# Two blocks of products opened together per arriving input tile, and one home for the split weights, in a two-block fp32 network on one core

## The reference

```python
def first_block(x, p, ...):
    u = rms_norm(h, norm_mix_w[l])
    proj = u @ w_in[l]                    # 24 blocks of 128 columns
    ...                                   # RG-LRU branch, GLA branch
    h = h + jnp.concatenate([ya, yb], axis=-1) @ w_out[l]
    gate = jax.nn.sigmoid(rms_norm(h, ple_norm_w[l]) @ w_ple_gate[l] + b_ple_gate[l])
    h = h + gate * (p[l] @ w_ple_proj[l])
...
# second block, per layer: n = rmsnorm(x, g); h = n * (1 + scale) + shift; x = x + gate * mixer(h)
def conv_branch(h, w_in, dw, db, ln_g, ln_b, w_out):      # layers 0 and 3
    a, b, gate = jnp.split(h @ w_in, 3, axis=-1)
    y = depthwise_conv(a * jax.nn.sigmoid(b), dw, db)
    y = jax.nn.silu(layernorm(y, ln_g, ln_b))
    return (y * jax.nn.silu(gate)) @ w_out
# layer 1: rwkv_mixer (features, wkv scan, readout @ w_o); layer 2: attn_mixer (q, k, v, g = h @ w_in;
# softmax attention; (o * silu(g)) @ w_out)
```

## Time and profile before

| | us |
|---|---|
| median of 3 runs | 3019.34 (3016.89 to 3021.15) |
| the profiled execution | 3007.58 |
| its span | 3005.8 |
| TensorE matmul busy | 2610.2 (87%) |
| VectorE busy | 1748.8 (58%) |
| ScalarE busy | 1122.0 (37%) |
| GpSimd busy | 776.2 (26%) |

### The profile page before, as it was taken

The page is one execution under the profiler, slowest core; times in us unless marked ns, Lnnn a source line. Parts: engine busy times, 40 slices in busy tenths (PEclk is TensorE's granted clock), DMA queues, the critical chain, the costliest instruction groups (busy, mean ns, idle before and its releaser), DMA issues. The chain is left out here.

```text
span 3005.8 us, 65971 instructions
## 1 busy us (share of the span) xinstructions
PE 2610.2 (87%) x28252; PEld 2028.2 (67%) x28252; DVE 1748.8 (58%) x2951; ACT 1122.0 (37%) x1751; POOL 776.2 (26%) x437
## 2 busy tenths in 40 slices
PE   7896879998599997788888888678999999898987
PEld 5774658776487686677677777567778755476755
DVE  4646978977822675454554554354771066535995
ACT  4531332223333422444444443332442344333323
POOL 2322210001122123644444452122332300032111
PEclk9998989989698898899999999889999999999998
DMA  4214424432234455111111100324332200033431
GB/s 149 77 43 133 161 71 118 111 93 91 97 107 151 157 188 182 40 36 45 51 40 46 51 25 14 122 91 147 133 126 64 84 1 1 1 119 92 136 94 56
DMA packets 83662, 266.34 MB, mean 89 GB/s; under 512 B 11824, under 2 KB 12848, under 8 KB 82992
## 3 DMA queue, kind: packets, MB, share of 16 engines
q1 hardware_dynamic: 74160, 236.97, 24.8%
q10 hardware_dynamic: 9216, 25.17, 2.1%
HBM read 203.04 MB, written 36.70 MB: 80 GB/s over the span
## 5 line engine op out<-in xcount | busy, mean ns | idle before, releaser
L358 PE MATMUL ps<-h_parts_conv,w_parts_conv 128*128 128x512 f32 x3936 | 766.5, 356 | 83.7 <-DVE h_parts_conv L344 47.6
L358 PEld LDWEIGHTS ps<-h_parts_conv,w_parts_conv 128*128 128x128 f32 x3936 | 643.2, 193 | 212.9 <-issue 54.7
L358 PE MATMUL ps<-scratch_scan 64*64 64x64 f32 (+1 forms) x15936 | 379.8, 239 | 82.9 <-issue 44.5
L358 PEld LDWEIGHTS ps<-scratch_scan 64*64 64x64 f32 x15936 | 342.9, 140 | 127.5 <-issue 83.6
L355 ACT ACTIVATE scratch_scan<-ps 128x384 f32<-128x384 f32 x560 | 241.0, 493 | 370.5 <-PE ps L358 228.4
L358 PE MATMUL ps<-h_parts_attn,w_parts_attn 128*128 128x512 f32 (+1 forms) x1536 | 330.5, 374 | 19.9 <-DVE h_parts_attn L352 12.3
L352 DVE SCALAR_TENSOR_TENSOR scratch_conv<-scratch_conv,vec 128x256 f32<-128x256 f32 (+1 forms) x672 | 335.2, 572 | 0.5
L358 PEld LDWEIGHTS ps<-h_parts_attn,w_parts_attn 128*128 128x128 f32 x1536 | 264.6, 191 | 78.6 <-issue 15.2
L432 POOL TENSOR_TENSOR w_parts_conv<-ring,w_parts_conv 128x1024 fp32r<-128x1024 f32 x50 | 131.4, 2629 | 592.2 <-ACT w_parts_conv L355 592.2
L358 PE MATMUL ps<-h_parts_block,w_parts_block 128*128 128x512 f32 x960 | 243.7, 414 | 38.5 <-POOL w_parts_block L432 27.7
L358 PEld LDWEIGHTS ps<-h_parts_block,w_parts_block 128*128 128x128 f32 x960 | 189.4, 200 | 92.4 <-issue 42.8
(11 more groups left out here) (206 smaller groups left out, 3586.0 us busy)
## 6 DMA issues: line engine op xcount, KB each, us to landing
ring<-in_weights SPq DMA_DIRECT2D x311, 512.0 KB, 3.7
rwkv_spill<-scratch_conv ACTq DMA_DIRECT2D x64, 384.0 KB, 2.3
stream<-rwkv_spill SPq DMA_DIRECT2D x64, 384.0 KB, 4.0
scratch_conv<-scratch_conv SPq DMA_DIRECT2D x128, 103.1 KB, 2.2
scratch_conv<-scratch_conv SPq DMA_DIRECT2D x128, 67.4 KB, 2.0
x_spill<-stream SPq DMA_DIRECT2D x2, 3072.0 KB, 9.7
y_spill<-scratch_scan SPq DMA_DIRECT2D x8, 384.0 KB, 4.0
scratch_rwkv_out<-y_spill SPq DMA_DIRECT2D x8, 384.0 KB, 6.5
```

Source lines behind the costliest of these rows:

```text
L358: return nc.tensor.matmul(o, l, r, start=start, stop=stop)
```

## The change

**1. Two blocks opened together.** A new function `first_products` takes the place of the first two `tile_product` calls in ten stages: in1, out1, gate1, conv0, convout0, rkvg, rwkvout, attn, conv1, convout1. At step k it waits for input tile k, does block 0's tile k, and then block 1's tile k - lag, with a lag of 4 at width 512 and of 3 at width 768. What stood between the two blocks (in attn the spreading, in gate1 a small product) now stands behind both. attnout keeps its order.

**2. One home for the split weights.** `weight_parts` makes the tensor once for everything to rkvg, is closed for the scan, and makes it again at rwkvout for all that follows. So the limits of gate1, rwkvout, attn and attnout now reach two blocks into the next stage: these are rounded and parted in the tail of the stage before.

```diff
         def memory(name, split, room=ROOM, width=TT):
             parts_scope.close()
             area_scope.close()
+            if not split:
+                w_scope.close()
+                PARTS.pop("W")
+            elif "W" not in PARTS:
+                weight_parts(name)
...
         def parts(name, tiles, width):
             PARTS["H"] = ap(parts_scope.enter_context(nc.sbuf_tensor(f"h_parts_{name}", [P, 2, tiles, width], F32R)))
-            PARTS["W"] = ap(parts_scope.enter_context(nc.sbuf_tensor(f"w_parts_{name}", [P, 2, 2, DT * P], F32R)))
+
+        def weight_parts(name):
+            PARTS["W"] = ap(w_scope.enter_context(nc.sbuf_tensor(f"w_parts_{name}", [P, 2, 2, DT * P], F32R)))
...
+        def first_products(pe, outs, width, fresh, lag):
+            j0 = done["take"]
+            done["take"] += len(outs)
+            Hh, Hl = PARTS["H"][:, 0], PARTS["H"][:, 1]
+            for step in range(DT + lag):
+                if step < DT:
+                    pe.wait_ge(fresh[0], fresh[1] + fresh[2] * (step + 1))
+                for i, o in enumerate(outs):
+                    k = step - lag * i
+                    if not 0 <= k < DT:
+                        continue
+                    if k == 0:
+                        pe.wait_ge(parted, j0 + i + 1)
+                    W = PARTS["W"][:, (j0 + i) % 2].rearrange("p e (k m) -> p e k m", k=DT)
+                    product(o, W[:, 0, k, :], Hh[:, k, :], width, k == 0, False)
+                    product(o, W[:, 0, k, :], Hl[:, k, :], width, False, False)
+                    last = product(o, W[:, 1, k, :], Hh[:, k, :], width, False, k == DT - 1)
+                    if k == DT - 1:
+                        last.then_inc(blocks_done, 1)
...
@@ add_products, TensorE (out1, convout0, rwkvout, convout1) @@
-                        tile_product(pe, PS[:, (m % 2) * 1024:(m % 2) * 1024 + width], width,
-                                     fresh=(split_low, base_low, 1) if split and m == 0 else None)
+                        if m == 0 and split:
+                            first_products(pe, [PS[:, 0:width], PS[:, 1024:1024 + width]], width, (split_low, base_low, 1), 4 if width == TX else 3)
+                        elif m >= 2 or not split:
+                            tile_product(pe, PS[:, (m % 2) * 1024:(m % 2) * 1024 + width], width)
...
@@ gate1, GpSimd and ACT @@
-                part_block(g, PSTART["gate1"] + DT)
+                part_block(g, PSTART["gate1"] + DT + 2)
...
-                    round_block(a, PSTART["gate1"] + min(m + 3, DT))
+                    round_block(a, PSTART["gate1"] + m + 3)
...
-        add_products("rwkvout", TT, lambda m, c: MODL[:, 1, 16 + m, c:c + 1], 0,
+        add_products("rwkvout", TT, lambda m, c: MODL[:, 1, 16 + m, c:c + 1], 2,
...
-        limit = PSTART["attnout"]
+        limit = PSTART["attnout"] + 2
...
@@ attn, TensorE @@
-                    tile_product(pe, o, TT if kind in "kv" else TX, fresh=input_fresh if n == 0 else None)
+                    if n == 0:
+                        first_products(pe, [o[:, 0:TX], PS[:, 1024:1024 + TX]], TX, input_fresh, 4)
+                    elif n >= 2:
+                        tile_product(pe, o, TT if kind in "kv" else TX)
                     if n == 0:
                         spread_conditions(pe, CB_PS, (0,))
...
@@ attnout, ACT and GpSimd @@
-                        round_block(a, min(PSTART["attnout"] + 2 * m + half + 3, PSTART["conv1"]))
+                        round_block(a, PSTART["attnout"] + 2 * m + half + 3)
...
-                part_block(g, PSTART["conv1"])
+                part_block(g, PSTART["conv1"] + 2)
```

More of the change, by code:

```diff
@@ L286, in C @@
             return CON[:, a:a + (CT[name][1] if n is None else n)]
-        kept_scope, area_scope, parts_scope = (ctx.enter_context(ExitStack()) for _ in range(3))
+        w_scope, kept_scope, area_scope, parts_scope = (ctx.enter_context(ExitStack()) for _ in range(4))
         AREA = {}
@@ L583, in layer_input @@
             return vector, scalar, (split_low, base_low, len(halves))
+        weight_parts("one")
         R1 = kept("r1", TX)
@@ L717, in _ @@
                         pe.wait_ge(bank_free, n - 1)
-                    tile_product(pe, bank(n % 2), TX, fresh=(split_low, base_low, 1) if n == 0 else None)
+                    if n == 0:
+                        first_products(pe, [bank(0), bank(1)], TX, (split_low, base_low, 1), 4)
+                    elif n >= 2:
+                        tile_product(pe, bank(n % 2), TX)
                     if 3 <= n < 7:
@@ L1095, in _ @@
                         pe.wait_ge(g_read, m - 1)
-                    tile_product(pe, PS[:, (m % 2) * 512:(m % 2) * 512 + 512], TX,
-                                 fresh=(split_low, base_low, 1) if m == 0 else None)
+                    if m == 0:
+                        first_products(pe, [PS[:, 0:512], PS[:, 512:1024]], TX, (split_low, base_low, 1), 4)
+                    elif m >= 2:
+                        tile_product(pe, PS[:, (m % 2) * 512:(m % 2) * 512 + 512], TX)
                     if m == 0:
@@ L1294, in _ @@
                                 pe.wait_ge(read, past + m)
-                            tile_product(pe, PS[:, part * 1024:part * 1024 + width], width,
-                                         fresh=input_fresh if m == 0 and part == 0 else None)
+                            if m == 0 and part == 0:
+                                first_products(pe, [PS[:, 0:width], PS[:, 1024:1024 + width]], width, input_fresh, 4 if width == TX else 3)
+                            elif m > 0 or part == 2:
+                                tile_product(pe, PS[:, part * 1024:part * 1024 + width], width)
                             if m >= 1 and part == 1:
@@ L1550, in _ @@
                             pe.wait_ge(ev, n - 2)
-                        tile_product(pe, area(), TT, fresh=(h_split, DT * e, 1) if m == 0 else None,
-                                     used=h_used if (kind, q, m) == prods[-1] and e + 1 < len(groups) else None)
+                        if n == 0:
+                            first_products(pe, [PS[:, 0:TT], PS[:, 1024:1024 + TT]], TT, (h_split, 0, 1), 3)
+                        elif n >= 2:
+                            tile_product(pe, area(), TT, fresh=(h_split, DT * e, 1) if m == 0 else None,
+                                         used=h_used if (kind, q, m) == prods[-1] and e + 1 < len(groups) else None)
                         n += 1
@@ L2772, in two_blocks @@
         parts_scope.close()
-        area("parts", "softmax", SPLIT)
+        area("parts", "softmax", SPLIT - 4 * DT * P)
         take = carve()
```

## The result

| | before | after |
|---|---|---|
| median of 20 runs each, us | 3020.59 | 3028.25 |
| lowest to highest | 3016.89 to 3030.01 | 3020.57 to 3034.77 |
| the profiled execution | 3007.58 | 3025.65 |
| its span | 3005.8 | 3023.9 |

The ratio is 1.0021, with a 95% interval of 1.0013 to 1.0029: 6.3 us slower (3.9 to 8.8).

The account below looks back on a forecast made before the run. TensorE, busy 87% of the span, bounds the kernel, leaving only its idle 13% or slower-clock time. Pairing 5.8 plus early weights 0.65 gave 6.45 us (0.21%): median 3012.9 us, 8-in-10 range 3001 to 3023.

Parts of the forecast that it names:

- the pairing: Openings of ten stages: block 1's tiles fill TensorE's waits between input arrivals, less new third-block waits; sum 5.8 us gained.
- Rival A: VectorE's run leaves gaps for GpSimd and the clock rises sooner: gain 14.3 us, median 3005.0; chance 0.27.
- the 1.5 us of the forecast: rkvg's gain from opening two blocks together, with GpSimd standing still until VectorE's run ends; bounds 0 and 4.8.
- Early weights: Weights prepared before the barrier: openings gain 12.3 us, tails lose 11.65, net +0.65.
- Openings: Gains from weights prepared earlier: conv0 2.8, attn 2.8, conv1 2.5, attnout 4.2 us; sum 12.3.
- Tails: Costs of preparing weights ahead of barriers: gate1 3.7, rwkvout 2.3, attnout 2.75, attn 2.9 us; sum 11.65.
- B: Rival: all ten third blocks come late or wait for ring slots, interleaving gives 0; median 3018.5; chance 0.20.
- C: Slower-side rival: in conv0 TensorE stays at half clock through paired tiles, 7.0 us slower, median 3026.3; chance 0.08.
- What would have shown it: Listed signs: conv0's third block near 412, GpSimd's rkvg operation over 4 us, tails 2.3 to 3.7 later, attn's third block later.

Follow-up runs that it names:

- second profile of the kernel before: The kernel before, unchanged, run once more with its own profile: ratio 1.0008 (0.9996 to 1.002), profiled execution 3022.15 us.
- experiment 3: Paired opening blocks alone in all ten stages, weights' place and limits as in the kernel before: 0.9993 (0.9978 to 1.0007), 2 us faster.
- experiment 7: Kernel before with W at the far place, remainder 0, and early weights at four more seams, no pairs: 1.0004 (0.9991 to 1.0017), 1.2 us slower.
- experiment 2: Kernel before with only the split weights' tensor moved to its place in the changed kernel: 1.0024 (1.0012 to 1.0036), 7.3 us slower.
- experiment 8: Kernel before with pairs only in conv0, convout0 and conv1, and attn's spreading ahead of its first product: 0.996 (0.9943 to 0.9978), 12 us faster.

## Why the prediction was wrong

**The step that failed** is the first sentence of the pairing, "The work is the same; what can be gained is tiles of block 1 that now lie between arrivals", and with it that the new home of W was costed at nothing, without a word. The matmuls are the same, their rate isn't. The place alone measured 7.3 us (3.6 to 10.9), and in the same place with remainder 0 it was gone (-5.7 to 1.8). A count agrees: 850 groups of three at 1.9 ns a matmul more are 4.8 us, and the mixed stretches some 3 us more than in the second profile of the kernel before. Such a count does not hold in every run (last section). With pairs -2.1, early weights +1.2 and place +7.3 the single parts add to 6.4 us, and the whole measured 6.3. That the two agree so closely is luck, as each part has an interval of some 4 us either way.

**Pairing: forecast 5.8, measured 2.1 (-2.1 to 6.6).** The interval just holds the forecast, so the total does not show an error here; the traces do, in two stages. The openings came close (kernel before, both profiles, against experiment 3; from the start of TensorE's last instruction ahead of the opening to the third block): conv0 35.6 to 32.3 us (3.3; forecast 2.9), convout0 34.1 or 35.1 to 32.0 (2 to 3, of which 1.1 went in the blocks behind; 2.5), conv1 22.2 to 21.6 (0.6; 0.5), attn's 1.4 to 2.3 us longer (2.3), in1, rwkvout and convout1 near 0 (0.5, -0.6, 0.8). rkvg was right up to the third block and wrong behind it. After the change, GpSimd, VectorE and TensorE there:

```profile
827.25 8.17 POOL L440 TENSOR_TENSOR w_parts_one<-ring,w_parts_one 128x1024 fp32r<-128x1024 f32 x2 [52.49 <-ACT w_parts_one L363]
```

```profile
822.32 8.56 DVE L360 SCALAR_TENSOR_TENSOR scratch_conv<-scratch_conv,vec 128x512 f32<-128x512 f32 x16
```

```profile
821.34 7.68 PE L366 MATMUL ps<-h_parts_conv,w_parts_one 128*128 128x512 f32 x42 [1.55 <-DVE h_parts_conv L352]
833.14 17.20 PE L366 MATMUL ps<-h_parts_conv,w_parts_one 128*128 128x512 f32 x87 [4.12 <-POOL w_parts_one L440]
```

VectorE's run ends at 830.88, and TensorE gets the weights at 833.14, 2.3 us later, exactly the reading of the earlier trace rows. Rival A had GpSimd get in between two of VectorE's instructions. That did not happen: at 0.53 us each, six of the run's sixteen started after 827.25, and none let it through. The Trainium skill ("SBUF — State Buffer", "Who interferes with whom") has the ports that the two engines share held by whoever issues first, for the whole instruction; here the trace shows GpSimd standing still not for one instruction but for the rest of the run. But TensorE now stands still for 4.1 us, and in the kernel with the pairs alone (4.24 us there) the granted clock after that is

```profile
828.30:834.90 6.60, 4.55 (x14) 0.50 0.45 135
```

0.50, with 14 matmuls in 4.55 us of work. Before, TensorE worked without a gap from 817.4 on, below full clock at first (the prediction had counted three tiles at half clock there) and at full clock from 826.0 on, so that the third block, from 830.7, had all of it:

```profile
817.40:826.00 8.60, 8.57 (x33) 0.65 0.12 48
826.00:840.00 14.00, 14.00 (x82) 1.00 0.30 103
```

The time from the start of the wait for the stage's first input to the end of its first eight blocks was 113.7 and 114.5 us before, 115.7 with the pairs: the 1.5 us of the forecast turned into a loss of 1.2 to 2.0. I had priced the new wait by its length alone. Whether the lower clock makes up the whole of it was not tested by itself.

**Early weights: forecast +0.65, measured -1.2 (-5.1 to 2.7).** Openings, experiment 3 against the changed kernel: conv0 2.9 (forecast 2.8), attn 2.9 (2.8), attnout 21.5 to 16.0, so 5.5 (4.2), conv1 1.2 (2.5): 12.5 for 12.3. Tails, from the last product to the next stage: gate1 8.9 to 12.7, so 3.8 (3.7), rwkvout 5.5 to 8.1, 2.6 (2.3), attnout 3.2 to 6.4, 3.2 (2.75). attn's cost 5.1 to 6.4 instead of 2.9. The start of softmax shows why. Before (the second profile):

```profile
2410.56 2.82 PE L358 MATMUL ps<-stream,scratch_attn 128*128 128x512 f32 x8 [0.94 <-PEq L2655]
```

and after, with the window from there:

```profile
2415.74 6.91 PE L366 MATMUL ps<-stream,scratch_attn 128*128 128x512 f32 x12 [3.92 <-PEq L2698]
```

```profile
2415.50:2421.00 5.50, 5.26 (x9) 0.50 0.00 0
```

The barrier is 3.0 us later, as forecast (2.9), and behind the longer stillness (3.92 us where it was 0.94) the clock is at 0.50, where it had been 1.00: two more us. It is the same omission as in rkvg. With the early weights alone (experiment 7) the stillness is the same, but the clock came back sooner, and attn's tail cost 3.1 to 4.4 us, not 5.1 to 6.4:

```profile
2408.14 4.24 PE L367 MATMUL ps<-stream,scratch_attn 128*128 128x512 f32 x8 [3.92 <-PEq L2665]
```

```profile
2408.00:2413.00 5.00, 4.24 (x8) 0.70 0.00 0
```

**The rivals.** None was right. A's mechanism did not occur. B (third blocks take it back) names what happened in rkvg and attn, and its time of no net gain lies nearest for the two parts without the place. C, the slower side, had the clock as its cause but in the wrong spot: conv0's pairs got the full clock, it was the new waits elsewhere that lost it. That C's side is the one that came is luck, since the largest part of the loss is W's place, which no rival has. The range, 3001 to 3023, left out 3028.25.

**What would have shown it** was half there: the tails that grow, attn's later third block and GpSimd's long operation in rkvg came as listed, and conv0's third block started at 419.5 in a stage that began 7.6 us later than before, so at 411.9 on the old scale, where 412 was forecast. That the busy time of TensorE could grow was not on the list.

## What to carry to other kernels

When a change moves a tensor that TensorE reads at full rate, note the places before and after, and compare the number of matmuls in a stretch without idle time. If it changed, try the same edit with the tensor some 64 bytes on before the edit itself is judged. A wait on TensorE is priced by its length and by the clock behind it, and preparations put ahead of a barrier cost what they save behind it unless they end before the other engines do.

## What the runs showed that was not expected

- A matmul of 512 columns followed the last by 226.7 ns when the inputs' and the weights' places were equal by 256 bytes, by 229.2, 232.6 and 233.3 when they differed by 64, 128 and 192, in near and far places alike (128 was tried in the near one only). In one execution attnout was fast beside a slow attn, by its own remainder. What makes it so is not shown; the runs show only that it takes both places together.
- The time did not always follow the rate. With remainder 64 and 192 bytes of padding the rate was slow and the time was not (1.0002, up to 1.0013; experiment 2, with the same rate, begins at 1.0012, on another chip). With remainder 128 the rate alone, 5.3 ns on 850 groups of three, would be some 13 us, and 5 were measured (1.5 to 9). What gives the time back is open, so the rate is the better witness of the place, and only the time says what it costs.
- Mixed stretches had two rates, 173.4 and 176.7 ns a matmul, in one and the same program: with remainder 0 in nine profiles 27% to 74% of the groups were slow; with 64 or 192 it was 64% in one and 81% to 98% in five; with 128 none was, and the mean was 175.5 ns. What chooses is open. Between the first two profiles of the kernel before, it makes a mean of 174.3 against 175.6 ns over 3942 matmuls, some 5 us of the 15 between them; the rest is not explained.
- The best version (experiment 8) leaves out the early weights and seven of the ten pairs. It was not combined with other remainders.
